# A hybrid decoder step in one kernel: state loads before output weights in the transfer queue, time steps in a bank of their own, and no wait for parameter rows before the second modulation tile

## The reference

```python
mod = (jax.nn.silu(c) @ w_ada[l] + b_ada[l])[:, None, :]
sh1, sc1, g1, sh2, sc2, g2 = jnp.split(mod, 6, axis=-1)
h = rmsnorm(x, norm1_w[l]) * (1 + sc1) + sh1
mix, cv, sm, sr, si = mixer(h, l, conv0[l], ssm0[l], s5r0[l], s5i0[l])
x = x + g1 * mix
h = rmsnorm(x, norm2_w[l]) * (1 + sc2) + sh2
x = x + g2 * moe_ffn(h, w_router, b_router, w1[l], w3[l], w2[l])
```

```python
dt = jax.nn.softplus(dt_raw.astype(f32) + dt_bias.astype(f32))
a = -jnp.exp(a_log.astype(f32))
y, new_ssm = ssd_scan(xs, dt, a, bm, cm, ssm_h0.astype(f32))
```

## Time and profile before

| what | value |
|---|---|
| median of three executions | 670.79 us (667.84, 670.79, 671.16) |
| the profiled execution: its time | 667.27 us |
| the profiled execution: span of its instructions | 665.5 us |
| between span and time | 1.8 us |
| mean granted TensorE clock | 0.969 of full speed |
| PE busy with matmuls | 606.5 us, 91% |
| DVE busy | 356.1 us, 54% |
| ACT busy | 150.2 us, 23% |
| POOL busy | 142.7 us, 21% |
| transfers | 178.55 MB, mean 268 GB/s |

### The profile page before, as it was taken

The page is one execution under the profiler, slowest core; times in us unless marked ns, Lnnn a source line. Parts: engine busy times, 40 slices in busy tenths (PEclk is TensorE's granted clock), DMA queues, the critical chain, the costliest instruction groups (busy, mean ns, idle before and its releaser), DMA issues. The chain is left out here.

```text
span 665.5 us, 8743 instructions
## 1 busy us (share of the span) xinstructions
PE 606.5 (91%) x3259; PEld 367.4 (55%) x3259; DVE 356.1 (54%) x926; ACT 150.2 (23%) x303; POOL 142.7 (21%) x242
## 2 busy tenths in 40 slices
PE   2779998999999999999799997699999999998994
PEld 1257776676766777656567774433434434434342
DVE  2897876888988734689762226501404404213036
ACT  3432435201000241323310014302101111011104
POOL 2300120599889115002010014100000000000000
PEclk9989999999999999999899999589999999998997
DMA  6989734033333180599978836499999999999932
GB/s 235 418 234 372 264 127 137 3 124 127 127 127 126 22 277 1 200 400 347 318 246 316 354 127 251 164 391 427 431 419 427 428 424 426 428 421 432 424 133 74
DMA packets 56188, 178.55 MB, mean 268 GB/s; under 512 B 9828, under 2 KB 27956, under 8 KB 47952
## 3 DMA queue, kind: packets, MB, share of 16 engines
q1 hardware_dynamic: 52596, 170.57, 66.3%
q0 software_dynamic: 1296, 4.72, 1.9%
q10 hardware_dynamic: 2252, 2.67, 1.3%
HBM read 170.56 MB, written 7.39 MB: 267 GB/s over the span
## 5 line engine op out<-in xcount | busy, mean ns | idle before, releaser
L674 PE MATMUL psum<-projection_region,ring 128*128 128x288 f32 x768 | 194.3, 411 | 5.2 <-DMA ring<-in_w_in 3.0
L674 PEld LDWEIGHTS psum<-projection_region,ring 128*128 128x128 f32 x768 | 144.9, 191 | 51.5 <-issue 8.7
L674 PE MATMUL psum<-ring,gate_region 128*64 128x512 f32 x400 | 107.5, 608 | 2.2 <-DMA mixer_region<-in_w 1.5
L1619 DVE TENSOR_TENSOR gate_region<-gate_region,psum 128x288 f32<-128x288 f32 (+1 forms) x16 | 12.0, 751 | 170.7 <-PE psum L674 148.8
L1300 ACT ACTIVATE gate_region<-psum 128x512 f32<-128x512 f32 (+1 forms) x66 | 36.2, 562 | 272.0 <-PE psum L674 173.3
L674 PE MATMUL psum<-mixer_region,gate_region 128*64 128x512 f32 x256 | 77.8, 594 | 0.0
L674 PEld LDWEIGHTS psum<-ring,gate_region 128*64 128x64 f32 x400 | 34.4, 140 | 69.4 <-issue 69.3
L1625 DVE SCALAR_TENSOR_TENSOR x_features<-psum,modulation,x_features 128x256 f32<-128x256 f32 x72 | 34.1, 473 | 25.5 <-PE psum L674 25.5
L674 PEld LDWEIGHTS psum<-mixer_region,gate_region 128*64 128x64 f32 x256 | 24.2, 137 | 22.1 <-issue 21.7
L658 POOL TENSOR_TENSOR gate_region<-group_key 128x1 f32<-128x1 f32 x8 | 1.9, 232 | 159.4 <-DVE gate_region L2182 153.8
L674 PE MATMUL psum<-gate_region 128*128 128x288 f32 x128 | 34.7, 414 | 0.0
(11 more groups left out here) (273 smaller groups left out, 778.7 us busy)
## 6 DMA issues: line engine op xcount, KB each, us to landing
ring<-in_w SPq DMA_DIRECT2D x25, 2048.0 KB, 23.0
mixer_region<-in_w SPq DMA_DIRECT2D x15, 2048.0 KB, 25.5
ring<-in_w_ada SPq DMA_DIRECT2D x12, 2048.0 KB, 10.9
ring<-in_w_in SPq DMA_DIRECT2D x10, 2048.0 KB, 11.8
projection_region<-in_w SPq DMA_DIRECT2D x4, 2048.0 KB, 22.4
tok_region<-in_w SPq DMA_DIRECT2D x4, 1536.0 KB, 25.2
ring<-in_w_glu SPq DMA_DIRECT2D x2, 2048.0 KB, 9.0
ring<-in_w_out_a SPq DMA_DIRECT2D x2, 2048.0 KB, 12.3
```

The lines of the kernel that those rows point to most:

```text
L674: return nc.tensor.matmul(out, lhsT, rhs, start=first, stop=last, skip_group_check=True)
L1619: return v.tensor_tensor(out, x, y, op)
```

## The change

Three edits.

1. In the loop over units, a pass stores before it loads, and the loads of pairs 5, 6 and 7 come one pass earlier: in pass 23 the store of pair 0, the load of pair 5, then unit 23; in pass 24 the store of pair 1, the load of pair 6, then unit 24; in pass 25 the store of pair 2, the load of pair 7, then unit 25.
2. The wait for the ten parameter rows ahead of unit 1 goes.
3. The time steps' products, copies and reads use bank 7 in place of bank 2. PE's wait for `pre_ok` ahead of the tails goes, and stands ahead of `s5_out(2)`, the first that writes bank 7.

```diff
             for n in range(N_UNITS):
-                if U_OUTA < n <= U_OUTA + KD - NH0:
-                    load_states(n - U_OUTA + NH0 - 1)
                 if U_OUTA <= n < U_OUTA + 5:
                     store_states(n - U_OUTA)
+                if U_OUTA <= n < U_OUTA + KD - NH0:
+                    load_states(n - U_OUTA + NH0)
                 if n >= NR:
                     sp.wait_ge(unit_used, n - NR + 1)
...
                 if n == 0:
                     sp.wait_ge(ld_c, 32)
-                elif n == 1:
-                    sp.wait_ge(ld_par, 16 * 10)
...
-                        last = mm(ps[32 * c:32 * c + 32, 2, 0:T], w_dt[:, 4 * r + c, :], hT[:, 4 * r + c, :], r == 0, r == 1)
+                        last = mm(ps[32 * c:32 * c + 32, 7, 0:T], w_dt[:, 4 * r + c, :], hT[:, 4 * r + c, :], r == 0, r == 1)
...
-                last = mm(ps[0:n, 2, i * H:(i + 1) * H], dt_sums[:, t0:t0 + n], sel9[:, 0:H], True, True)
+                last = mm(ps[0:n, 7, i * H:(i + 1) * H], dt_sums[:, t0:t0 + n], sel9[:, 0:H], True, True)
...
             pe.wait_ge(s5w_ok, 2)
-            pe.wait_ge(pre_ok, 1)
             pe.wait_ge(tails_ok, XT)
...
                 pe.wait_ge(s5_h, 2 * p + 2)
+                if p == 2:
+                    pe.wait_ge(pre_ok, 1)
...
-                        f(dt_sums, ps[:, 2, 0:T]).then_inc(dt_ps, 1)
+                        f(dt_sums, ps[:, 7, 0:T]).then_inc(dt_ps, 1)
...
-            link(tt(dt3[:, 0:2, :], ps[:, 2, 0:2 * H].rearrange("p (i h) -> p i h", h=H),
+            link(tt(dt3[:, 0:2, :], ps[:, 7, 0:2 * H].rearrange("p (i h) -> p i h", h=H),
...
-            tt(dt3[0:TS, 2, :], ps[0:TS, 2, 2 * H:3 * H], dtb[0:TS, :], ALU.add).then_inc(pre_ok, 1)
+            tt(dt3[0:TS, 2, :], ps[0:TS, 7, 2 * H:3 * H], dtb[0:TS, :], ALU.add).then_inc(pre_ok, 1)
```

## The result

The changed kernel takes 673.15 us (median of 15 executions, 670.47 to 676.57), the kernel before, in turns with it on the same chip, 669.88 (15 executions, 666.75 to 674.74). The ratio is 1.0045, with a 95% interval from 1.0023 to 1.0067: about 3.0 us slower, 1.5 to 4.5. This ratio is not the quotient of the two medians, which would be 1.0049 (3.3 us); further down the two differ by up to 0.2%. In a later series of 12 executions the ratio was 1.0066 [1.0038, 1.0095], 4.4 us. The prediction said 4.2 us slower and 675.0. Of the 1.85 us between 675.0 and 673.15, 0.91 come from the median that it started from, 670.79 where 15 executions gave 669.88. The total was right. Where the time went was right only in part, and that is the subject here.

A forecast was written before the change was run, and what follows sets the result against it. The end was taken to hang on the stream of expert tiles, which moves with whatever ends the earlier stages. Terms 0.4 + 0 + 3.8 = +4.2 us on 667.27 gave 671.5; from the median 670.79, 675.0; range 668.5 to 680.

The forecast's parts named there:

- The sum: Whole kernel: the terms of the three edits, 0.4 + 0 + 3.8, make it 4.2 us slower than the profiled execution.
- Edit 1, +3.8: Late state loads: the load of pair 7 lands at 328.2 where it was 324.4, 3.8 us later.
- rounds: SP's queue of late state loads: load, unit and store issued together, SP waiting for the store; 12.2 us each.
- the lower bound of 10.8: Late state loads: shortest time allowed for one load, unit and store, 7.8 + 3.0 us; the upper was 13.5.
- The rival of short rounds: Late state loads: under 10.6 us per load, unit and store, taken 9.8; pair 7's load lands 2.4 us earlier; chance 0.13.
- The fit: Late state loads: a transfer takes 2.0 us plus its bytes at 436 GB/s; the change would then win 3.2 us.
- Edit 3, 0: Tails and S5 products: PE's 2.75 us stall goes, but PE waits 2.6 us longer for DVE; effect 0.
- the clock behind it: Rival at the S5 products: after the 3.5 us idle PE runs at half speed for some 3.4 us, costing 1.7; chance 0.14.
- Edit 2, +0.4: Start: parameter rows come 2.1 us later, so the first projection tile starts at 37.9, 0.4 us later.
- bounds 1.1 and 3.0: Start: parameter rows delayed 1.1 us if spread over 16 engines, 3.0 us if held by 8.
- wrong if the first tile started near 36: Start: sign against the forecast, which put the first projection tile near 37.9 with no wait for unit 4.

The follow-up runs named there:

- the filled kernel: The changed kernel plus 6 matmuls nobody reads where PE stood idle before the products of S5 steps 2 and 3; ratio 1.0025 to the kernel before, +1.7 us.

## Why the prediction was right, and where it was not

**The sum** was +4.2 us, the measurements are +3.0 and +4.4. The first is 0.45%, just inside the 0.5% that was called no change, the second 0.66%, outside it. Both medians, 673.15 and 673.59, lie in the range of 668.5 to 680.

**Edit 1, +3.8.** Alone it costs +4.2 and +4.4 us, with rounds of 12.3 to 12.4 where the forecast worked out 12.2. That pair 7 came at 328.17 and 328.24 where it said 328.2 is partly luck: the store of pair 0 was issued 0.4 and 0.7 us later than in the profile before, rounds were longer than said and the load's landing shorter. The idea was right: a store that is the only thing in the queue, then a load, a unit and the next store behind it, with SP waiting for the last. The run with the units out of the relay shows that the unit is the long link. In the changed kernel itself the step failed in its size: rounds of 10.9 to 11.1, and only 0.2 and 1.0 us more from the store of pair 0 to pair 7. Two terms were off there: a round was taken as 12.2 and measured 11.0, near the lower bound of 10.8, and a load's landing as 5.0 and measured 4.1. The forecast had added a unit of 8.7 us and 3.2 for the packets of load and store. The round that was looked at closely with edit 1 alone shows another split: the unit had landed 9.0 us behind its issue, and 1.5 us went to a straggling end of the store. So a nearly right sum stood on terms that were partly wrong. The rival of short rounds set its border at 10.6, and it was missed by 0.3. The fit that the forecast took from the Trainium skill (DMA: Bandwidth & Descriptors, Anatomy of one DMA) gave an estimated 9.2 us for a round, and 10.9 to 12.7 were measured. That section states the fit for transfers that GpSimd issues, and these are SP's, which the forecast leaves out.

**Edit 3, 0.** This is the step that failed. "PE waits 2.6 us longer, about 3.5 in one piece": measured 3.40, exactly the idle time that was said. "What is late next is DVE": right, the S5 products started when they had. But "so the term is 0" left out that idle time has a price of its own, the clock behind it. That was put among the rivals, with a chance of 0.14 and a price of 1.7 us. It came in four profiles of four, and cost 3.3 us against the profile of before, 2.0 against the mean of the bank 2 kernels. The four kernels without this idle time, in which the clock stays, show the cause. The price was worked out with 3.4 us at half clock, an estimate from a row at the start; in the changed kernel it lasted from about 126.5 to 133.5, twice as long. The forecast also took for granted that the old wait of 2.75 us left the clock alone, from one profile. In three of six profiles it did not.

**Edit 2, +0.4.** The parameters were expected 2.1 us later (bounds 1.1 and 3.0); over all profiles it is 1.6, in the first pair of profiles 0.65, below the lower bound. By the forecast's own terms that bound puts the first tile at 35.8 + 1.1 = 36.9, 0.6 us earlier than before, and not 0.4. The first tile came at 36.6 to 38.0, forecast 37.9, and the effect on the time, -0.5 with an interval from -2.4 to +1.5, holds +0.4 too. That DVE and no longer unit 4 would start it was right, but in four of the eight profiles without edit 2 DVE starts it too. By the forecast's own words it was wrong if the first tile started near 36, and 36.59 in the first profile was close to that; the later ones put it higher.

**So the total held partly by luck**: in the profiled pair, edit 1 was 3.6 us cheaper than said, edit 2 0.75 cheaper and edit 3 3.3 dearer. The three edits alone add up to about +4.3 - 0.5 + 0.8 = +4.6 (means of two series for edits 1 and 3), near the changed kernel's +3.0 and +4.4. Where in the changed kernel the difference goes from execution to execution, its two profiles show: span 668.9 with the clock at 0.962, and 673.1 at 0.957, the second with a low clock for some 10 us behind pair 7 and not 3.

**What stays open**: why the store of a round ends late in edit 1 alone and in the filled kernel (six rounds of six), and not in the changed kernel (four of four), with the same list of transfers. Why the half clock behind the 3.4 us lasted some 6.8 us in both profiles of the changed kernel and 3.4 in both of edit 3 alone. And how much of a median's +4.4 belongs to the relay when its rounds are short.

## What to carry to other kernels

A wait that is taken from one place and appears whole at another is not free: ask what PE does behind it, and look at the granted clock there. Put work into the gap, or move other work so that it closes. When a buffer must be stored before it is loaded again, count the links of that relay and what lies between them: issue stores as soon as their data is there, and keep large transfers out of the round. And one profile shows one execution: before a difference of 3 us is explained, the same stretch of several kernels that share it is worth laying side by side.

## What the runs showed of the hardware

The lower clock behind a wait is not fixed by its length. Behind the wait of 2.75 us before the tails it fell in three profiles of six, with the instructions around it the same; behind 3.4 us in four of four; behind the 3.2 to 7.4 us for pair 7 in ten of ten, and in three of the four kernels without that wait it fell between 323 and 326 us all the same, behind two waits under 1 us (0.82 and 0.70). How long it stayed differed too: some 3, 7, 10 or 14 us behind waits that were alike. The differences between the executions of one kernel go with it. Of 34 executions of the kernel before, the four shortest (666.07 to 666.78 us) had a mean granted clock of 0.967 to 0.970, and the four longest (673.26 to 674.46) 0.952 to 0.957; the correlation of clock and time over the 34 is -0.88.

A store of 512 KB landed 1.5 us later (11.3 us for 9.8) when its last nine packets straggled, with the other transfers of the round taking the same time (9.0 and 9.1 us for the unit, 4.1 for the load).

Small loads beside a full queue of large packets lose more than the first profile showed: the ten parameter rows came 0.8 to 2.2 us later in six profiles.
